# Sample attention scores of a hybrid decoder step, laid out by head first instead of by sequence first

## What is computed

```python
s = jnp.einsum('bqhd,bkhd->bhqk', qb, k).astype(jnp.float32) * scale
s = jnp.where(k_pos[None, :] <= qp[:, None], s, -jnp.inf)
a = jax.nn.softmax(s, axis=-1).reshape(B, H, 2, qb.shape[1], Lk)
w = a[:, :, 0] - lam * a[:, :, 1]
return jnp.einsum('bhqk,bkhv->bqhv', w, v32)
```

## Time and profile before

| | |
|---|---|
| median of 3 runs | 2361.03 us (2356.24 to 2362.98) |
| profiled execution, its own time | 2358.5 us |
| span of its trace, first to last instruction | 2356.7 us |
| instructions | 43259 |
| TensorE matmuls, busy | 2273.2 us, 96% of the span |
| VectorE, ScalarE, GpSimd, busy | 995.4, 667.4 and 1139.1 us |
| mean granted clock of TensorE | 0.992 |

### The profile page before, as it was taken

One profiled execution on the slowest core, in us unless ns is written; L12 is line 12 of the kernel. 1 busy time (PEld: TensorE's weight loads), 2 busy tenths in 40 slices (PEclk: granted clock), 3 DMA queues, 4 the chain that ended last, 5 costly groups with the idle time before them and its releaser, 6 DMA issues.

```text
span 2356.7 us, 43259 instructions
## 1 busy us (share of the span) xinstructions
PE 2273.2 (96%) x17964; PEld 2171.9 (92%) x17964; DVE 995.4 (42%) x1253; ACT 667.4 (28%) x1004; POOL 1139.1 (48%) x765
## 2 busy tenths in 40 slices
PE   7999999999999999999999999999989999999998
PEld 7988998877999999999998989888789999999997
DVE  3263845632454444313616356366134534442134
ACT  3222213331133222222423031224111332222234
POOL 4464555544744444444646455455457334444444
PEclk9999999999999999999999999999999999999998
DMA  5523224234242332233343232421432333222331
GB/s 138 141 55 78 78 47 127 65 108 126 81 125 84 89 89 87 74 85 103 84 119 94 55 93 55 105 83 53 133 108 86 114 90 88 83 84 80 85 96 56
DMA packets 371387, 213.76 MB, mean 91 GB/s; under 512 B 34306, under 2 KB 356966, under 8 KB 370738
## 3 DMA queue, kind: packets, MB, share of 16 engines
q1 hardware_dynamic: 369714, 205.11, 32.0%
q10 hardware_dynamic: 1536, 6.69, 0.8%
HBM read 195.88 MB, written 15.88 MB: 90 GB/s over the span
## 4 chain that ended last, share of the span: by engine, by line
PE 85%; DVE 5%; POOL 3%; issue 2%; DMA 2%; ACT 2%; SPq 1%; POOLq 0%; DVEq 0%; ACTq 0%
PE G L626 73%; PE M L1867 1%; PE M L1795 1%; POOL wL L572 1%; POOL wH L566 1%; DMA h<-spill 1%; PE M L1860 1%; PE M L1826 1%; PE M L713 1%; DMA d_V<-in_cache_v 1%; POOL sq L682 1%; PE M L1282 0%; DVE MG L1944 0%; PE M L1591 0%; PE M L1265 0%
## 5 line engine op out<-in xcount | busy, mean ns | idle before, releaser
L626 PE MATMUL G<-xH,wH 128*128 128x272 f32 x3616 | 776.9, 296 | 23.8 <-DMA d_V<-in_cache_v 7.8
L626 PE MATMUL G<-xH,wL 128*128 128x272 f32 x3616 | 751.3, 289 | 0.0
L626 PE MATMUL G<-xL,wH 128*128 128x272 f32 x3616 | 748.9, 289 | 0.0
L618 POOL TENSOR_TENSOR wL<-raw,wH 128x1024 fp32r<-128x1024 f32 (+2 forms) x186 | 420.7, 2262 | 596.6 <-ACT wH L2038 290.4
L626 PEld LDWEIGHTS G<-xH,wH 128*128 128x128 f32 x3616 | 569.4, 189 | 57.1 <-issue 29.6
L626 PEld LDWEIGHTS G<-xL,wH 128*128 128x128 f32 x3616 | 571.3, 190 | 0.0
L626 PEld LDWEIGHTS G<-xH,wL 128*128 128x128 f32 x3616 | 568.1, 190 | 0.0
L566 POOL TENSOR_TENSOR wH<-raw,ones 128x512 fp32r<-128x512 f32 x240 | 268.7, 1141 | 501.1 <-PE G L626 501.1
L572 POOL TENSOR_TENSOR wL<-raw,wH 128x512 fp32r<-128x512 f32 x240 | 334.6, 1415 | 9.4
L546 ACT ACTIVATE wH<-raw 128x1024 fp32r<-128x1024 f32 (+2 forms) x116 | 105.9, 913 | 320.3 <-PE G L626 299.0
L2038 ACT ACTIVATE wH<-raw 128x1024 fp32r<-128x1024 f32 x82 | 87.1, 1062 | 325.6 <-PE G L626 325.6
(11 more groups left out here) (365 smaller groups left out, 2836.1 us busy)
## 6 DMA issues: line engine op xcount, KB each, us to landing
raw<-in_w_in SPq DMA_DIRECT2D x72, 512.0 KB, 3.9
raw<-in_w_gate SPq DMA_DIRECT2D x48, 512.0 KB, 3.9
raw<-in_w_ffn_gate SPq DMA_DIRECT2D x44, 512.0 KB, 3.8
raw<-in_w_ffn_up SPq DMA_DIRECT2D x44, 512.0 KB, 3.8
raw<-in_w_branch SPq DMA_DIRECT2D x24, 512.0 KB, 3.5
raw<-in_w_ffn_down SPq DMA_DIRECT2D x32, 384.0 KB, 3.4
raw<-in_w_ffn_down SPq DMA_DIRECT2D x32, 320.0 KB, 3.2
d_kr<-in_cache_k SPq DMA_DIRECT2D x32, 256.0 KB, 2.7
```

What stands on the lines that cost most here:

```text
L618: pool.tensor_tensor(wL[n % SPLIT][:, 0:kb(j), :], raw[n % RAW][:, 0:kb(j), :], wH[n % SPLIT][:, 0:kb(j), :].bitcast(F32), ALU.subtract).t ...
L626: mm = pe.matmul(G[:, slot, half, 0:HALF], w[n % SPLIT][:, wk, :], x[:, xk, half * HALF:(half + 1) * HALF], start=(start and at == 0 and w ...
```

## The change

The rows of the scores become 32hd + 8j + 4c + t: head first. A query block is still 128 x 32, but its 8 columns that are not zero are now those of the sequence `j`, and each head's matmul writes to its own 32 rows. The four sequences of a group add up in place, so the bank is started at `j == 0` and stopped at `j == 3`. `query(g, j, hd)` reads `d_qbd` with a stride of `QB = 136` elements for each sequence, by which the same copies put the 8 columns at offset 8j of the block. The matmuls of a sequence come in another order: four against the past keys, then four against the sample keys. The mask is added at `j == 0` alone, by four matmuls, one for each head, through `ident8`, a 128 x 32 selection of columns of the identity that VectorE makes once at the start. The views of the two `tensor_reduce` forms name the axes in the new order. The numbers of matmuls of each size are as before.

```diff
+        ident8 = fixed.put("ident8", [P, NS])
...
-        d_qbd = t.put("d_qbd", [P, DEC_BATCH, HEADS, 2, DEC_SEQ * HEADS])
+        QB = 4 * NS + 2 * DEC_SEQ
+        d_qbd = t.put("d_qbd", [P, DEC_BATCH * QB])
...
+            dve.tensor_copy(ident8[:, :].rearrange("p (j x) -> p j x", j=4),
+                            consts_in[:, 0, :].rearrange("p (j x) -> p j x", j=4)[:, :, 0:2 * DEC_SEQ])
...
-                pool.memset(d_qbd[:, :, :, :, :], 0.0).then_inc(s.qbd_ready, 1)
+                pool.memset(d_qbd[:, :], 0.0).then_inc(s.qbd_ready, 1)
...
-                        q0 = hd * 2 * DEC_SEQ + m * DEC_SEQ
-                        flat = d_qbd[lo64[m], :, hd, :, :].rearrange("p b x y -> p b (x y)")
+                        q0 = hd * NS + m * DEC_SEQ
+                        flat = d_qbd[lo64[m], :].rearrange("p (b z) -> p b z", z=QB)
...
-                        v = M[:, 1, pg * P:(pg + 1) * P].rearrange("p (j h c t) -> p j h t c", j=4, h=HEADS, c=2)
+                        v = M[:, 1, pg * P:(pg + 1) * P].rearrange("p (h j c t) -> p j h t c", j=4, h=HEADS, c=2)
...
-                    v = M[0:NS, 1, 2 * P:3 * P].rearrange("p (j h c t) -> p j h t c", j=4, h=HEADS, c=2)
+                    v = M[0:NS, 1, 2 * P:3 * P].rearrange("p (h j c t) -> p j h t c", j=4, h=HEADS, c=2)
...
+                def rows_of(hd):
+                    return slice(NS * hd, NS * (hd + 1))
+
+                def query(g, j, hd):
+                    at = g * 4 * QB + (j * HEADS + hd) * NS
+                    return d_qbd[:, at:at + NS]
...
-                        rows = slice(32 * j, 32 * (j + 1))
                         for hd in range(HEADS):
-                            q = d_qbd[:, b, hd, :, :].rearrange("p x y -> p (x y)")
-                            pe.matmul(M[rows, 0, 0:2 * PAGE], q, d_KT[:, hd, :], start=(hd == 0), stop=False,
-                                      skip_group_check=True)
-                            pe.matmul(M[rows, 0, 2 * PAGE:2 * PAGE + NS], q, C[:, 4 + hd, SEQ:T], start=False, stop=False,
-                                      skip_group_check=True)
-                        mm = pe.matmul(M[rows, 0, 2 * PAGE:2 * PAGE + NS], ident[:, 32 * j:32 * (j + 1)], sneg[:, g, :],
-                                       start=False, stop=True, skip_group_check=True)
+                            mm = pe.matmul(M[rows_of(hd), 0, 0:2 * PAGE], query(g, j, hd), d_KT[:, hd, :], start=(j == 0),
+                                           stop=(j == 3), skip_group_check=True)
+                        for hd in range(HEADS):
+                            own = M[rows_of(hd), 0, 2 * PAGE:2 * PAGE + NS]
+                            mm = pe.matmul(own, query(g, j, hd), C[:, 4 + hd, SEQ:T], start=False, stop=(j == 3),
+                                           skip_group_check=True)
+                            if j == 0:
+                                mm = pe.matmul(own, ident8[:, :], sneg[:, g, :], start=False, stop=False, skip_group_check=True)
                         mm.then_inc(s.ss_ps, 1)
```

## The result

The changed kernel took 2332.34 us (median of 4 runs, 2329.59 to 2333.95), the kernel before 2362.01 beside it (median of 4, 2356.24 to 2365.31). The medians lie 29.7 us apart. The ratio that is used here, with its 95% interval, is 0.9889 (0.9869 to 0.9910): 26 us less, between 21 and 31. The forecast was 22.4 us less. All ratios leave out the slow executions, one of ten of the kernel with old rows (7687 us) and one of five of that with gates and clears (12289 us).

What follows compares the result with a forecast made beforehand. TensorE was taken as the bound. A group of four sequences falls from 8.56 to 2.95 us, saving 5.61, or 22.4 over two groups and two layers: 2361.0 - 22.4 = 2338.6 us, range 2332 to 2350.

Steps and rivals of the forecast that it cites:

- The bound: Score matmuls of the sample attention: TensorE is the limit, no other engine on the path; 2.14 us a sequence, 34.2 us.
- Four abreast: Page products of a sequence: four heads' strips run together as in the value products, 0.55 us instead of 1.84.
- The short products: Four sample-key products a sequence: 0.15 us, between 0.06 and 0.24; four mask matmuls a group: likewise 0.15.
- sign for the transposes: Timeline mark of being right: transposes start 0.75 to 0.9 us behind a sequence's first page product, where it was 2.2.
- up to a few tenths: Second group of each layer: VectorE's outputs could show this much per layer; counted as zero, 1 us in the range.
- at worst: First group: VectorE's 7.8 us wait for the scores loses 5.6, leaving 2 us at the least.
- GpSimd, DMA, ScalarE: Weight splits, key pages and page copies stay hidden; GpSimd keeps 4 to 5 us of waiting; value-page stalls move along.
- `ident8`: One more small VectorE copy at 30 us, covered by VectorE's next wait of 3.36 us; uncovered at most 1.4 us, once.
- The clock: Layer 2's fill behind the longer value-page stall: part at 1.2 instead of 2.4 GHz; each time 1.2 us, either way.
- Pairs: Page products: only neighbouring heads overlap, five rounds, 1.20 us a sequence; saving 12.0, time 2349; chance 0.10.
- The wait rival: Shorter sequences meet weight splits, a page or VectorE's outputs; with two thirds of the gain kept, 2354 us; chance 0.08.
- Paying for each change of strip: Score matmuls: eight strip changes a sequence at 0.27 us each, 35 us more in all, 2396 us; chance 0.04.

Runs made afterwards that it cites:

- old rows: Kernel before with its layout, all four heads of a sequence in one strip, but four page products first, then four short ones: ratio 1.0001.
- gates and clears: Changed kernel with ScalarE's two gate sigmoids two pages earlier and VectorE's two weight clears ahead of its wait for the first group's scores: ratio 0.9885.
- Head by head: Changed kernel's layout with the matmuls in the old order, past keys and sample keys of one head, then of the next: ratio 0.9902.
- three orders: Changed kernel with gate sigmoids and clears earlier and the first group's prompt-output split behind two outputs: 2328.06 us, ratio 0.9858.
- three kernels with moved gates: Changed kernel with ScalarE's second-group gate sigmoids earlier: alone 0.9900, with VectorE's clears earlier 0.9885, as three orders 0.9858.

## Why the prediction was right

**The number.** The three comparisons gave 26, 23 and 24 us where 22.4 was forecast. The first median, 2332.34, lies only 0.3 us inside the range, whose lower end was 2332; that it isn't outside is luck. The mechanism doesn't hang on it, since the blocks on the chain were measured by themselves.

**The bound.** "Nobody else stands in it": TensorE's matmuls were the path in 14 of the 16 sequences, and doubling the page products came back as time. Right.

**Four abreast.** Taken from the value products, half as wide, with half the weight columns. The page products took 0.57 us where 0.55 was forecast. The rows of a neighbour that already used the strips were worth more here than any duration of the line itself.

**The short products.** Forecast 0.15 for four and measured 0.06; the mask 0.15 and measured 0.10. They overlap as the long ones do: eight records start between 500.37 and 500.42. The Trainium skill ("TensorE: Matmul & The Clock Gate", section "Back-to-back issue gap") gives a floor of about 25 ns between matmuls of 1 to 64 columns. By an estimate from it eight records would take 0.2 us; they took 0.06, so between strips it doesn't hold here. The prediction's sign for the transposes, 0.75 to 0.9 us behind the first page product, was too high for the same reason: it is 0.73 in the first sequence of a group and 0.63 in the others. For a group the blocks are 4 x 0.57 + 0.16 + 3 x 0.06 = 2.62 us, and up to 0.05 more where the chain ends at the last short product. The saving is 5.9 a group and 23.8 in all, 1.4 over the forecast.

**VectorE.** The prediction named it as nearest and expected "up to a few tenths" in each layer from its outputs in the second group. It was 0.1 to 0.2, by the chain. In the first group VectorE's wait went from 7.8 to 4.7 us, well above the 2 "at worst".

**GpSimd, DMA, ScalarE.** GpSimd's waits went from 57 to 47 us and no page was late. One split waited 5.3 us for its weights in the changed profile without standing in the chain. The value pages' stalls, 3.1 to 3.3 us and once 4.6 before, are 3.1 to 3.6 in the first profile of the changed kernel, and the second has one of 4.63 again. So they moved along, within their scatter.

**`ident8`.** One copy of 1.32 us at 30.4, but the cast behind it, which took 1.37 before, then took 0.21. It wasn't free for that: the product behind the casts (line 2193), 0.21 before, then took 1.37:

```profile
30.38 1.32 DVE L509 COPY ident<-consts_in 128x32 f32<-128x32 f32 x1
31.61 0.21 DVE L511 CAST bigR<-consts_in 128x128 fp32r<-128x128 f32 x1
31.75 0.21 DVE L512 CAST negR<-consts_in 128x128 fp32r<-128x128 f32 x1
31.89 1.37 DVE L2193 TENSOR_TENSOR lamp<-lamv 128x64 f32<-128x64 f32 x1
```

The second profile of the changed kernel and that of the old rows, which has no `ident8`, reach this stretch at the same time (29.93 and 29.92). VectorE is done with it at 34.61 in the first and at 33.42 in the second, so it costs 1.2 us. VectorE's next wait takes that up, 2.12 us instead of 3.35, and its first product of layer 1 starts at 36.73 and 36.78. It was covered, as forecast. Why single instructions take 1.3 us there wasn't tested. The copy and the product end 0.06 to 0.09 us behind an instruction of GpSimd (line 686) that runs beside them.

**The clock.** It was counted as 1.2 us either way for each dip. The six dips of the first pair of profiles cost 1.2 to 1.6 us each, three on either side, and cancel. That they did was luck.

**The rivals.** Pairs: 1.2 us a sequence was not seen. But the rule of the Trainium skill behind that rival ("TensorE: Matmul & The Clock Gate", section "The mechanism"), "pc-monotone in start AND end", is half alive. Head by head, later page products start 0.4 us ahead of the first short product in the second sequence of a group, against the rule; in the first sequence the next strip's product did wait, until 500.71. The wait rival took 0.2 to 0.4 us in all, where its time asked for 15. Paying for each change of strip is refuted at 0.57 us for eight records in four strips.

## What to carry to other kernels

When small-row products run one behind the other, look at which rows of PSUM neighbours write to: in different 32-row strips they shared the time of one here, and the cost was the passes of the fullest strip. The order counts with the layout: put the long products of all strips next to each other and the short ones behind. And when a stretch on the path gets shorter, move the work of the other engines that was placed by its old length.

## What the runs showed of the hardware that was not expected

- TensorE's reach past a busy strip is short. Two waiting records of 32 columns, behind the strip's second page pass and with their weight loads, were passed and four were not, and with four the sequence went from 0.65 to 2.06 us. With four the next strip's product started together with the first of them, so past the three that were left. What exactly is full then was not tried.
- VectorE's scaling of 288 columns (line 1751) took 0.38 us in the changed kernel at 552.38 and 1.28 in the one with three orders at 552.08. GpSimd's split ran until 551.86 in the first and until 553.18 in the second. The same holds in both layers of the three kernels with moved gates: six times the scaling starts while a split runs, takes 1.26 to 1.28 us and ends about 0.17 us behind it, and everywhere else it starts with no split running and takes 0.38. That the one holds up the other was not tested by itself. It gives back 0.9 us a layer of what the earlier gates save.
